# Activations stationary and 512 weight columns streamed in a two-layer float32 kernel

## The reference

```
h = rms_norm(x, norm_g);  proj = h @ w_in
ya, yb, yc = band attention, RWKV-7 time mix, memory attention, each times silu(...)
merged = sigmoid(ga)*(ya @ w_up_a) + sigmoid(gb)*(yb @ w_up_b) + sigmoid(gc)*(yc @ w_up_c)
x = x + merged @ w_o
h = rms_norm(x, norm1);  proj = h @ w_in_2
mixed = g0*(o_a @ w_br_attn) + g1*(o_g @ w_br_gla) + g2*(y_c @ w_br_conv)   # g = sigmoid(merge columns)
x = x + mixed @ w_out
h2 = rms_norm(x, norm2)
x = x + (silu(h2 @ w_ffn_gate) * (h2 @ w_ffn_up)) @ w_ffn_down
out = rms_norm(x, final_norm)
```

## Time and profile before

| what | value |
|---|---|
| median of 3 runs | 3304.81 us (3304.29 to 3305.22) |
| span of the profiled execution | 3304.2 us |
| PE busy | 96% of the span, 25642 matmuls |
| PEld, DVE, ACT busy | 94%, 52%, 42% |
| DMA | mean 155 GB/s |

### The profile page before, as it was taken

How to read it: one execution, slowest core, us unless ns; L and a number is a source line. 1 busy time by engine, 2 the same in 40 slices (tenths; PEclk the granted TensorE clock), 3 DMA queues, 4 the chain that set the end, 5 groups by cost and what they waited for, 6 DMA issues and landing times.

```text
span 3304.2 us, 60057 instructions
## 1 busy us (share of the span) xinstructions
PE 3188.2 (96%) x25642; PEld 3122.3 (94%) x25642; DVE 1712.7 (52%) x1954; ACT 1382.2 (42%) x1527; POOL 100.0 (3%) x230
## 2 busy tenths in 40 slices
PE   6999999999999999999999999999998999999997
PEld 6999999989999999999999989999998999999997
DVE  5455555547555555645455456555445444444444
ACT  4333343434444344434344434444434444444332
POOL 3000000000100000000000000000000000000000
PEclk9999999999999999999999999999999999999999
DMA  5333333335566554555555645566554556565553
GB/s 149 99 103 103 103 109 103 103 97 173 171 192 184 155 154 145 174 164 161 170 162 171 182 128 146 170 182 187 181 162 149 183 178 185 175 191 182 180 176 116
DMA packets 353558, 512.12 MB, mean 155 GB/s; under 512 B 18161, under 2 KB 137157, under 8 KB 352597
## 3 DMA queue, kind: packets, MB, share of 16 engines
q1 hardware_dynamic: 352596, 506.11, 50.9%
q0 software_dynamic: 768, 3.20, 0.4%
HBM read 507.13 MB, written 2.11 MB: 154 GB/s over the span
## 4 chain that ended last, share of the span: by engine, by line
PE 93%; DVE 4%; ACT 1%; issue 1%; SPq 0%; DMA 0%; POOL 0%; DVEq 0%; ACTq 0%
PE gp L1263 27%; PE gp L1264 27%; PE gp L1265 27%; PE ps L1422 1%; PE ps L1389 1%; PE ps L1437 1%; PE ps L1440 1%; PE ps L1317 1%; DVE w_lo L824 1%; PE ps L1343 1%; PE ps L1302 1%; PE ps L1368 1%; DVE arena L933 1%; PE ps L1329 1%; DVE arena L818 0%
## 5 line engine op out<-in xcount | busy, mean ns | idle before, releaser
L824 DVE TENSOR_TENSOR w_lo<-w_raw,w_hi 128x1024 fp32r<-128x1024 f32 (+2 forms) x976 | 1165.5, 1203 | 1168.1 <-ACT w_hi L528 1166.8
L1263 PE MATMUL gp<-h_hi,w_hi 128*128 128x256 f32 x5920 | 1713.5, 289 | 30.3 <-DVE h_lo L916 21.0
L1264 PE MATMUL gp<-h_lo,w_hi 128*128 128x256 f32 x5920 | 1684.5, 285 | 0.0
L1265 PE MATMUL gp<-h_hi,w_lo 128*128 128x256 f32 x5920 | 1684.5, 285 | 0.0
L528 ACT ACTIVATE w_hi<-w_raw 128x1024 fp32r<-128x1024 f32 (+2 forms) x976 | 1007.6, 1039 | 1244.9 <-PE gp L1265 1223.4
L1263 PEld LDWEIGHTS gp<-h_hi,w_hi 128*128 128x128 f32 x5920 | 1146.0, 194 | 45.9 <-issue 34.7
L1264 PEld LDWEIGHTS gp<-h_lo,w_hi 128*128 128x128 f32 x5920 | 1145.8, 194 | 1.7
L1265 PEld LDWEIGHTS gp<-h_hi,w_lo 128*128 128x128 f32 x5920 | 1144.8, 193 | 0.0
L1265 PE MATMUL gp<-y_hi,w_lo 128*128 128x256 f32 x896 | 253.7, 283 | 0.0
L1263 PE MATMUL gp<-y_hi,w_hi 128*128 128x256 f32 x896 | 252.9, 282 | 0.0
L1264 PE MATMUL gp<-y_lo,w_hi 128*128 128x256 f32 x768 | 216.9, 282 | 0.0
(11 more groups left out here) (273 smaller groups left out, 2055.4 us busy)
## 6 DMA issues: line engine op xcount, KB each, us to landing
w_raw<-in_w_in SPq DMA_DIRECT2D x384, 512.0 KB, 3.7
w_raw<-in_w_ffn_gate SPq DMA_DIRECT2D x88, 512.0 KB, 4.4
w_raw<-in_w_ffn_up SPq DMA_DIRECT2D x88, 512.0 KB, 4.3
w_raw<-in_w_ffn_down SPq DMA_DIRECT2D x88, 512.0 KB, 3.7
w_raw<-in_w_in SPq DMA_DIRECT2D x136, 256.0 KB, 3.3
w_raw<-in_w_in SPq DMA_DIRECT2D x128, 192.0 KB, 2.8
w_raw<-in_w_mem_kv SPq DMA_DIRECT2D x32, 512.0 KB, 3.7
w_raw<-in_w_o SPq DMA_DIRECT2D x32, 512.0 KB, 4.3
```

The costliest lines, as they stand in the source:

```text
L824: dve.tensor_tensor(w_lo[:, slot, 0:size], w_raw[:, slot, 0:size], w_hi[:, slot, 0:size].bitcast(F32), ALU.subtract)\
L1263: pe.matmul(o, wh, x_hi[k], start=(k == 0 and c % 2 == 0), stop=False, skip_group_check=True)
L1264: pe.matmul(o, wh, x_lo[k], start=False, stop=False, skip_group_check=True)
L1265: ins = pe.matmul(o, wl, x_hi[k], start=False, stop=(k == last_k), skip_group_check=True)
```

## The change

A new kind of unit, "rows", has the same 128x1024 weights, but its operands are swapped. The stationary operand is a 128x128 tile of the activation (half `a` of the positions), and 512 weight columns stream past it. A unit has 2 k-tiles x 2 halves x 3 products, 12 matmuls of 512 columns, and the output arrives in rows: positions on partitions. All gate blocks, branch projections (`up`), `w_o`, `w_out_2` and the feed-forward blocks become "rows": 616 of the 976 units. The RWKV, attention, memory, LoRA, GLA and convolution columns stay as they were.

The residual `xr` and the merged activation `mg` are now in rows. What the next product needs as its stationary operand must have its k dimension on partitions, so PE turns it (`turn_rows`): 8 transposes of 128x128 into half of `ps` (`cross`), which ACT rounds (`cross_high`) and DVE splits (`cross_low`). That happens for 4 pieces of each of three norms, for 4 pieces of the merged activation twice, and for 11 pieces of the feed-forward product, after unit `TURN_AT` = 1 of a later block. Row statistics come from ACT's accumulating squares (`row_sums`), and the gains are loaded broadcast over the partitions. The transposes of the input into `x_t`, those of the output and the multiplications by ones are gone. `gate_3` is split: its four gates first (`sig_3`), then the four projections (`up_3`). All loops are unrolled.

```diff
-KINDS = {"wide": (2, 4), "pair": (2, 4), "trio": (2, 3), "narrow": (4, 1)}
-DMAS = {"wide": 1, "pair": 2, "trio": 2, "narrow": 1}
+Block = namedtuple("Block", "weight kt kind col operand evac arg")
+KINDS = {"wide": (2, 4), "rows": (2, 4), "pair": (2, 4), "trio": (2, 3), "narrow": (4, 1)}
...
+    def rows(w, col, n, operand, evac, kt=KD):
+        return wide(w, col, n, operand, evac, kt, "rows")
 
     def gated(w, gate_col, up, evac):
-        return [b for j in range(2) for b in (
-            Block(w, KD, "wide", 0, gate_col + 512 * j, 1024, "h", "gate", 2 * j),
-            Block(up, KB, "wide", 0, 512 * j, 1024, "y", evac, 2 * j + 1))]
-    phase("lora", [Block("w_in", KD, "narrow", 0, LORA_COL, 0, "h", "lora", 0)])
+        return [b for j in range(4) for b in (
+            Block(w, KD, "rows", gate_col + 512 * j, "h", "gate", j),
+            Block(up, KB, "rows", 512 * j, "y", evac, j))]
...
+    phase("gate_c", rows("w_in", GC_COL, 4, "h", "gate_c"))
+    phase("up_c", rows("w_up_c", 0, 4, "y", "merge_c", KB))
+    phase("o", rows("w_o", 0, 4, "h", "residual"))
...
+    phase("gate_3", rows("w_in_2", M_COL + 4096, 4, "h", "gate_3"))
+    phase("up_3", rows("w_br_conv_2", 0, 4, "y", "merge_3", KB))
+    phase("o2", rows("w_out_2", 0, 4, "h", "residual"))
+    phase("ffn", [b for i in range(NF) for b in (
+        Block("w_ffn_gate_2", KD, "rows", 512 * i, "h", "ffn_gate", i),
+        Block("w_ffn_up_2", KD, "rows", 512 * i, "h", "ffn_up", i))])
+    phase("ffn_down", rows("w_ffn_down_2", 0, 4, "f", "residual", KF))
...
+TURN_AT = 1
+CROSS = {"norm_g": 0, "merged": 4, "norm1_w_2": 8, "merged_2": 12, "norm2_w_2": 16, "ffn": 20}
...
+            x_in = dram["x"].rearrange("b (a p) d -> p (b a) d", p=P)
+            for j in range(4):
+                sp.dma_start(piece(xr, j), piece(x_in, j)).then_inc(sem(f"x_landed{j}"), 16)
+            def load_gain(name):
+                src = dram[name]
+                sp.dma_start(gain[:], bass.AP(src.tensor, src.offset, [[0, P], [1, D]])).then_inc(sem("gain_landed"), 16)
+            load_gain("norm_g")
...
+                if name in ("o", "o2", "ffn_down"):
+                    sp.wait_ge(sem("norm_rows"), 4 * ("o", "o2", "ffn_down").index(name) + 4)
+                    load_gain({"o": "norm1_w_2", "o2": "norm2_w_2", "ffn_down": "final_norm_w_2"}[name])
+                run(unit, name)
...
+            def cross_high(dst):
+                seen.need("cross_turned")
+                act.activation(dst, cross[(seen.n["cross_turned"] - 1) % 2], ACT.Copy).then_inc(sem("cross_hi"), 1)
+            def row_sums(j, sq, ready):
+                ready(j)
+                act_n["sums"] += 1
+                if act_n["sums"] > 1:
+                    act.wait_ge(sem("row_sums"), act_n["sums"] - 1)
+                for a in range(2):
+                    ins = act.activation(sq[:, a, :], xr[:, a, 512 * j:512 * j + 512], ACT.Square, scale=D ** -0.5,
+                                         accum_out=stat[:, 4 * a + j:4 * a + j + 1])
+                ins.then_inc(sem("row_sums"), 1)
...
+            def norm_high(fill, k):
+                cross_high(tiles4(h_hi, 0))
+                cross_high(tiles4(h_hi, 1))
+                fill(k)
+                cross_high(tiles4(h_hi, 2))
+                fill(k)
+                cross_high(tiles4(h_hi, 3))
+            def up_and_project(up, project, sq):
+                m0, m1 = phases[up][0], phases[project][0]
+                for m in range(m0, m1 + 4):
+                    for n in block_units(m):
+                        unit(n)
+                        if n == first[m] + TURN_AT and m0 < m <= m1:
+                            cross_high(tiles4(h_hi, m - m0 - 1))
+                    if m >= m1:
+                        row_sums(m - m1, sq, lambda j: wait_evacuated(act, m1 + j))
+                row_root()
...
+                elif kind in ("merge", "merge_c", "merge_3"):
+                    if kind == "merge":
+                        wait_evacuated(dve, m - 1)
+                        gate = sig
+                    else:
+                        gate = (sig_c if kind == "merge_c" else sig_3)[:, a * UNIT:(a + 1) * UNIT]
+                    dve.tensor_tensor(prod, gate, g, ALU.mult).then_inc(done, 1)
+                    wait_evacuated(dve, m)
+                    dve.tensor_tensor(piece(mg, a), piece(mg, a), halves(prod), ALU.add).then_inc(sem("added"), 1)
                 elif kind == "residual":
-                    part = flat(x_t[:].rearrange("p a b -> p (a b)"), a * UNIT, i, body * UNIT)
-                    dve.tensor_tensor(part, part, g, ALU.add).then_inc(done, 1)
+                    dve.tensor_tensor(piece(xr, a), piece(xr, a), halves(g), ALU.add).then_inc(done, 1)
                 elif kind == "ffn_up":
-                    wait_evacuated(dve, m - 1, i, body)
-                    dve.tensor_tensor(f_t[:, 1, :], f_t[:, 0, :], g, ALU.mult).then_inc(sem("ffn_prod"), 1)
-                    dve.wait_ge(sem("ffn_hi"), on(i, 1, 1))
-                    hi_part = flat(f_hi[:].rearrange("p a b -> p (a b)"), 0, i, UNIT)
-                    lo_part = flat(f_lo[:].rearrange("p a b -> p (a b)"), 0, i, UNIT)
-                    dve.tensor_tensor(lo_part, f_t[:, 1, :], hi_part.bitcast(F32), ALU.subtract).then_inc(done, 1)
+                    wait_evacuated(dve, m - 1)
+                    dve.tensor_tensor(f_t[:, 1, :], f_t[:, 0, :], g, ALU.mult).then_inc(done, 1)
...
+            def cross_low(dst, rounded):
+                seen.need("cross_hi")
+                dve.tensor_tensor(dst, cross[(seen.n["cross_hi"] - 1) % 2], rounded.bitcast(F32), ALU.subtract).then_inc(sem("cross_lo"), 1)
...
+            def norm(fill, k):
+                def scaled(j):
+                    for a in range(2):
+                        ins = dve.scalar_tensor_tensor(n_x[j % 2][:, a, :], xr[:, a, 512 * j:512 * j + 512], stat[:, 8 + a:9 + a],
+                                                       gain[:, 512 * j:512 * j + 512], ALU.mult, ALU.mult)
+                    ins.then_inc(sem("norm_rows"), 1)
+                def low(j):
+                    cross_low(tiles4(h_lo, j), tiles4(h_hi, j))
+                row_scales()
+                inverse_root(stat[:, 8:10])
+                seen.need("gain_landed", 16)
+                scaled(0)
+                scaled(1)
+                low(0)
+                low(1)
+                fill(1)
+                scaled(2)
+                fill(k - 1)
+                scaled(3)
+                low(2)
+                fill(k)
+                low(3)
...
+            def scale_piece(j):
+                seen.need("row_sums")
+                for a in range(2):
+                    part = xr[:, a, 512 * j:512 * j + 512]
+                    ins = dve.tensor_tensor(part, part, gain[:, 512 * j:512 * j + 512], ALU.mult)
+                ins.then_inc(sem("rows_scaled"), 1)
+            for m in range(m0, m1 + 4):
+                for n in block_units(m):
+                    if n >= first[m0] + 4:
+                        unit(n)
+                    if n == first[m] + TURN_AT and m0 < m <= m1 and (m - m0) % 2 == 0:
+                        i = (m - m0) // 2 - 1
+                        cross_low(tiles4(f_lo, i), tiles4(f_hi, i))
+                if m == m1 + 1:
+                    seen.need("gain_landed", 16)
+                if m > m1:
+                    scale_piece(m - m1 - 1)
+            seen.need("row_sums")
+            dve.tensor_reduce(stat[:, 8:10], stat[:, 0:8].rearrange("p (a b) -> p a b", b=4), AX, ALU.add).then_inc(sem("row_mean"), 1)
+            seen.skip("row_sums", -1)
+            scale_piece(3)
+            seen.need("root_ready")
+            dve.reciprocal(stat[:, 8:10], stat[:, 8:10]).then_inc(sem("root_final"), 1)
+            seen.need("root_final")
+            dve.wait_ge(sem("rows_scaled"), 4)
+            dve.tensor_scalar(xr[:, 0, :], xr[:, 0, :], stat[:, 8:9], None, ALU.mult).then_inc(sem("out_ready0"), 1)
...
+                    if b.kind == "rows":
+                        wh, wl = (w[:, slot, j * 512:(j + 1) * 512] for w in (w_hi, w_lo))
+                        for a in range(2):
+                            o = gp[:, s, a * 512:(a + 1) * 512]
+                            xh, xl = (x[k][:, a * P:(a + 1) * P] for x in (x_hi, x_lo))
+                            pe.matmul(o, xh, wh, start=(k == 0), stop=False)
+                            pe.matmul(o, xl, wh, start=False, stop=False)
+                            ins = pe.matmul(o, xh, wl, start=False, stop=(k == last_k))
+                        continue
...
+            def turn_rows(e, src):
+                if e >= 2:
+                    pe.wait_ge(sem("cross_lo"), e - 1)
+                for c in range(4):
+                    for a in range(2):
+                        ins = pe.transpose(cross[e % 2][:, c * T + a * P:c * T + (a + 1) * P], src[:, a, c * P:(c + 1) * P], ident[:])
```

(51 more changed lines are left out.)

431 lines of the change are left out of this document (172 added, 259 removed).

## The result

The changed kernel took 3228.99 us (median of 4 runs, 3224.02 to 3232.64), the kernel before 3305.01 beside it: a ratio of 0.9772, 95% interval 0.9758 to 0.9786. It is faster by 76 us where 189 were forecast, and it lies 11 us above the forecast range. The profiled execution has a span of 3230.9 us against 3304.2, so the traces have 73.3 us to explain.

A forecast was written before the change was run, and what follows sets the result against it. PE was taken as the bound, through its matmul pace. Terms -174.0 + 7.5 - 6.5 - 4.1 - 1.2 - 10 = -188.3 against the median 3304.81 gave 3116 us; range 3092 to 3218.

The forecast's parts named there:

- Second, the nearest row.: Pace g of a 512-column product, taken from plain float32 matmuls of 256 columns: 0.216 us, the weight load fully hidden.
- rival B: All 512-column products: 0.013 us above the columns stays once per matmul, g = 0.2267, total 3194; chance 0.24.
- The slow clock: Sign from 256-column matmuls at 1.2 GHz: they take exactly their 0.213 us, so nothing is added per matmul.
- small terms: All terms but the product pace: helpers +7.5, start -6.5, `o2` -4.1, norms -1.2, end -10 us, some with bounds.
- A: Main case for the 512-column products: g = 0.216, total 3116, own range 3092 to 3138; chance 0.50.
- rival D: In the 512-column products weight loads are no longer hidden: g = 0.325, about 3908; slower above g = 0.242; chance 0.05.
- 604 units of 512-column products: Converted units at full clock: 12 x 0.216 = 2.592 us each instead of 2.88, saving 0.288 each, -174.0 us.
- PE's helpers: PE's own extra work: nine statistics batches removed, -15.5, and 23 transposing turns added, +23.0; net +7.5 us.
- start: Before the first product, now at 39.19 us: a new chain ends at 31.5, taken as -6.5 us (bounds -3 and -9).
- `o2` entry: Ahead of `o2`: PE's 4.1 us wait for four splits in a row goes, as they lie beside blocks, -4.1 us.
- two norms between stages: PE's 12.0 us gap between `o` and `Q`: new chain of 11.2, -0.6 at each norm, -1.2 us (bounds -4 and +3).
- end: After the last product: 25.4 us become 15.5, of which 7.5 chain and 8 stores, -10 us (bounds -6 and -13).

The follow-up runs named there:

- pace: Whole computation left out, input copied to output; PE alone runs rows of 12 to 48 matmuls of one form: 0.2267 us for 512 aligned float32r columns.
- after_aligned: Changed kernel with `stat` moved behind the two activation tensors, so `h` is back on a multiple of 256 B relative to the weights: 3204.34 us, ratio 0.9698.
- all_aligned: Changed kernel with `stat` behind the activation tensors and 24 elements of padding, so `y` and `f` are aligned to 256 B too: 3191.15 us, ratio 0.9659.
- loads: Whole computation left out; PE alone, stationary tiles of 128 to 32 columns, rows of 400: with 64 stationary, 0.230 us for 512 streamed columns, 0.1133 for 256.
- before_shift: Kernel before with 64 B of unused padding ahead of `h_hi`: 3269.06 us beside 3302.20, ratio 0.9899.

## Why the prediction was wrong

**The step that failed: "Second, the nearest row."** It took g = 0.216 from plain float32 matmuls of 256 columns, as "the time of 512 columns", and concluded: "So a load hides fully behind a stream of that length." `pace` shows that a record of that type spends two columns' time on each column (0.429 us for 512), so the row tells what that type adds to its own stream, 0.0025 us, and nothing about float32r. A float32r stream of the same time, 512 columns, starts 0.2267 apart at best: 0.0133 us per matmul remain above the columns, as for 320, 384 and 256. That is rival B's term, 12 x 0.0107 x 604 = 78 us of the lost gain. B had "none streams at the full rate as these do" beside it, and 0.24. The rate alone is not what parts the types: bf16 streams at the full rate, with a load in each, and adds 0.0025 (0.2158). What does is not shown. The slow clock, which I held against B, speaks truly (0.213) but says nothing about the fast one.

**What no case had: addresses.** In the changed kernel 512 columns take 0.2333 and not 0.2267, 12 x 0.0066 x 604 = 48 us. Of that about 34 us belong to the products on `h`, 70% of them, which the 64 B of `stat` had moved (`after_aligned`); the same 64 B gave some back on the 256-column ones. The other 14 belong to `y` and `f`, which lay at a difference of 24 elements in the kernel before as well, where 512 columns take 0.2333 (`all_aligned`). B with aligned operands was to be 3194; `all_aligned` has 3191.15. That B's number fits is partly luck, since its small terms differ.

**The sums.** With the bounds that the prediction states for its small terms (-3, +3 and -6) B ends at 3206 and A at 3128; its 3218 and 3138 do not follow from them. Its chain between `o` and `Q` ends at 11.2, which is 0.8 less than 12.0, not 0.6. Neither changes the outcome.

**The break-even of rival D** was right in kind: the pace decides everything, and 0.242 was never near.

**The other terms**, forecast and measured:

| term | forecast | measured |
|---|---|---|
| 604 units of 512-column products | -174.0 | -48.3 (12 x 0.2333 = 2.800) |
| PE's helpers | +7.5 | +4.7 (a turn costs 0.79 and 0.09 at the next product) |
| start | -6.5 | -6.1 at the first product, -4.3 by the first RWKV head |
| `o2` entry | -4.1 | -4.1 (no wait left) |
| two norms between stages | -1.2 | -2.1 (10.8 us each) |
| end | -10 | -12.4 (13.0 us; 6.2 of chain, 6.8 of stores) |
| 256-column products, granted clock and all else | 0 | the rest, -6.8 |

With -4.3 for the start the measured column adds up to the 73.3 us of the spans, since the last line is what remains. It is no measurement: 0.0024 us less in some 7,000 products would be -17, of which part lies in stages where PE waits for a chain, as `before_shift` showed. Against it stands the granted clock, 0.982 over the span where the kernel before has 0.984: 58 us less than full against 53, so up to 5 us (an estimate). The mechanisms of the small terms were right: the reduction, the table load, the two scalings and the transposes stand in the trace in the order in which the prediction put them, and SP's wait for `norm_rows` and the DMA rate (187 GB/s for the 202 feared) cost nothing.

**What stays open** is why a matmul of this type takes more than its columns. It depends on both lengths and on the difference of addresses, which suggests that stream and weight load meet at the same memory, but `loads` refutes the simple form (a narrower load is no cheaper under 512 columns). Nor is it known what chooses between 0.113 and 0.118 for 256 columns at a difference of 16 or 48, only that the choice holds for a whole unbroken stretch of products. All these paces are at full clock.

## What to carry to other kernels

Take the pace of a new matmul from a row of the same type, not from one with the same time. Ask of the row how many columns per second it streams, but do not stop there: bf16 streams as fast as float32r and paces at 0.2158 where float32r takes 0.2267 and more. When a pace is a few per cent above its columns, move the operands against each other before restructuring anything; here 64 B more made one kernel 33 us faster, and 64 B less made the other 25 us faster, both with some share of the granted clock in it. A change that adds a small tensor moves everything behind it: compare the pace of instructions that were not changed, which tells at once whether layout has entered the result.

## What the runs showed that I had not expected

- Float32r products pace by the difference of operand addresses modulo 256 B: 0.2267 to 0.2342 us for 512 columns, 0.1133 to 0.1201 for 256, with PE alone and in the full kernel alike. At some differences there are two paces, and an unbroken stretch of products keeps one of them.
- The best difference for one length is among the worst for the other: 0 gives 0.2267 for 512 columns and 0.120 for 256.
- DVE, ACT and DMA work did not slow a product: 0.120, 0.2333 and 0.2267 are the same beside it and without.
- The granted clock over the span differs between kernels: 0.980 to 0.981 in the runs of `before_shift`, 0.984 to 0.987 in those of `all_aligned`. An estimate of what 0.005 can be worth is 16 us, as much as some of the effects sought.
- A tile that is already stationary, given again, saves nothing, and 512 columns with 64 stationary ones are slower (0.230) than with 128 (0.2267).
